# Handing seven of eight residual additions at five stage boundaries from VectorE to GpSimd

## The reference, cut to what matters

```
for l in range(2):                                   # first_block
    h = rmsnorm(x, norm_mix_pre[l])
    merged = ...                                     # pooling, convolution, attention, gates
    x = x + rmsnorm(merged @ w_out[l], norm_mix_post[l])
    h = rmsnorm(x, norm_mem_pre[l])
    x = x + rmsnorm(memory_cross_attention(h, ...), norm_mem_post[l])
    h = rmsnorm(x, norm_ffn_pre[l])
    y = (silu(conv(ua)) * ub) @ w_down[l]
    x = x + rmsnorm(y, norm_ffn_post[l])
```

## Time and profile before

| | us |
|---|---|
| median of three runs | 4000.37 |
| lowest and highest | 3993.73, 4000.42 |
| the profiled execution: time | 4001.47 |
| the profiled execution: span | 3999.7 |
| PE busy of the span | 3786.9 |
| DVE busy | 2063.7 |
| ACT busy | 1287.0 |
| POOL busy | 1203.3 |

### The profile page before, as it was taken

The page is one execution under the profiler, slowest core; times in us unless marked ns, Lnnn a source line. Parts: engine busy times, 40 slices in busy tenths (PEclk is TensorE's granted clock), DMA queues, the critical chain, the costliest instruction groups (busy, mean ns, idle before and its releaser), DMA issues. The chain is left out here.

```text
span 3999.7 us, 49029 instructions
## 1 busy us (share of the span) xinstructions
PE 3786.9 (95%) x19420; PEld 3183.6 (80%) x19420; DVE 2063.7 (52%) x3416; ACT 1287.0 (32%) x2149; POOL 1203.3 (30%) x548
## 2 busy tenths in 40 slices
PE   8999998999999998899989998899999889999999
PEld 6777776888777787688867777799999778877887
DVE  5547646565644773565456665623343566633112
ACT  4332244222433323422234443311111335543223
POOL 2224433444322443244421111122222210123443
PEclk8999999999999999999999997999999999999999
DMA  3224422333212442233321101233332200112332
GB/s 105 64 59 135 125 77 66 116 100 103 82 56 65 126 133 74 74 106 100 111 73 38 28 26 38 69 95 111 95 108 88 62 19 16 28 48 75 94 95 84
DMA packets 544449, 316.71 MB, mean 79 GB/s; under 512 B 35876, under 2 KB 517215, under 8 KB 544223
## 3 DMA queue, kind: packets, MB, share of 16 engines
q1 hardware_dynamic: 525184, 277.39, 23.9%
q10 hardware_dynamic: 19039, 36.19, 2.9%
HBM read 311.44 MB, written 2.10 MB: 78 GB/s over the span
## 5 line engine op out<-in xcount | busy, mean ns | idle before, releaser
L459 POOL TENSOR_TENSOR wlo<-wraw,whi 128x1024 fp32r<-128x1024 f32 (+6 forms) x544 | 1203.1, 2216 | 2774.9 <-ACT whi L452 2774.6
L475 PE MATMUL acc<-hh,whi 128*128 128x512 f32 (+2 forms) x2744 | 1064.1, 388 | 32.1 <-DVE hl L635 24.5
L476 PE MATMUL acc<-hl,whi 128*128 128x512 f32 (+2 forms) x2744 | 1034.7, 377 | 0.0
L477 PE MATMUL acc<-hh,wlo 128*128 128x512 f32 (+2 forms) x2744 | 1034.2, 377 | 0.0
L452 ACT ACTIVATE whi<-wraw 128x1024 fp32r<-128x1024 f32 (+6 forms) x544 | 523.7, 965 | 652.2 <-DMA wraw<-in_w_up 184.9
L475 PEld LDWEIGHTS acc<-hh,whi 128*128 128x128 f32 x2744 | 521.8, 190 | 146.8 <-issue 31.2
L476 PEld LDWEIGHTS acc<-hl,whi 128*128 128x128 f32 x2744 | 521.8, 190 | 91.5 <-issue 12.3
L477 PEld LDWEIGHTS acc<-hh,wlo 128*128 128x128 f32 x2744 | 521.0, 190 | 83.9
L1543 DVE TENSOR_TENSOR t<-acc,sq 128x768 f32<-128x768 f32 (+1 forms) x44 | 36.3, 825 | 444.3 <-PE acc L477 444.3
L475 PE MATMUL ob<-hh,whi 128*128 128x512 f32 (+3 forms) x576 | 214.3, 372 | 6.8 <-DVEq L831 6.6
L475 PE MATMUL acc<-act1h,whi 128*128 128x512 f32 x528 | 209.7, 397 | 1.4 <-DVE act1l L1551 1.4
(11 more groups left out here) (412 smaller groups left out, 6232.4 us busy)
## 6 DMA issues: line engine op xcount, KB each, us to landing
wraw<-in_ffn_w SPq DMA_DIRECT2D x120, 512.0 KB, 3.8
wraw<-in_w_in SPq DMA_DIRECT2D x102, 512.0 KB, 3.9
wraw<-in_w_up SPq DMA_DIRECT2D x88, 512.0 KB, 3.8
ada_w<-in_ada_w ACTq DMA_DIRECT2D x64, 512.0 KB, 4.1
ada_w<-in_ada_w SPq DMA_DIRECT2D x32, 512.0 KB, 4.2
wraw<-in_w_down SPq DMA_DIRECT2D x32, 512.0 KB, 4.0
wraw<-in_w_out SPq DMA_DIRECT2D x16, 512.0 KB, 4.1
wraw<-in_w_mkv SPq DMA_DIRECT2D x16, 512.0 KB, 4.0
```

The costliest lines, as they stand in the source:

```text
L459: e.tensor_tensor(wlo[0:rows, s, a:b, 0:w], wraw[0:rows, s, a:b, 0:w], whi[0:rows, s, a:b, 0:w].bitcast(F32), ALU.subtract).then_inc(lo_re ...
L475: e.matmul(o, wh, xh, start=first, stop=False)
L476: e.matmul(o, wh, xl, start=False, stop=False)
L477: return e.matmul(o, wl, xh, start=False, stop=last)
```

## The change

In the five boundaries that have a y, DVE no longer adds features 1 to 7. It makes the scaled y (`t2`) and the low half (`hl`) as before, and still adds feature 0. POOL adds the other seven, reading `t2` and `xres` and writing `xres`. Two semaphores are new: `t_scaled` tells POOL that a `t2` is there, `x_added` tells ACT that a feature is added, and tells DVE that a `t2` buffer is free again. POOL's additions come in its program after the low halves of the next stage's first two slabs and ahead of the third's. What the additions compute is the same.

```diff
+        t_scaled, x_added = sem("t_scaled"), sem("x_added")
...
+        def ends_here(T, tiles, waits, ahead=2):
+            stage_ends[len(slabs) + ahead] = (T, tiles, waits)
+
+        def pool_adds(e, c, T, tiles, waits):
+            for k in tiles:
+                e.wait_ge(t_scaled, c.next(t_scaled, waits))
+                e.tensor_tensor(xres[:, k, 0:T], xres[:, k, 0:T], t2[:, k % 2, 0:T], ALU.add).then_inc(x_added, 1)
...
-        def act_boundary(e, c, g, half=None):
+        def act_boundary(e, c, g, half=None, added=LATER):
...
-                e.wait_ge(x_ready, c.next(x_ready))
+                done = x_added if k in added else x_ready
+                e.wait_ge(done, c.next(done))
...
                 if k < KT and y is not None:
+                    if k == 2:
+                        e.wait_ge(x_ready, c.at(x_ready, 0))
+                    if k >= 3:
+                        e.wait_ge(x_added, c.next(x_added))
                     e.scalar_tensor_tensor(out=t2[:, k % 2, 0:SEQ], in0=y[:, k, :], scalar=G(k), in1=ysum[:, 0:SEQ],
-                                           op0=ALU.mult, op1=ALU.mult).then_inc(dve_step, 1)
+                                           op0=ALU.mult, op1=ALU.mult).then_inc(t_scaled if k else dve_step, 1)
+                if k == 0 and y is not None:
                     e.wait_ge(dve_step, c.next(dve_step))
                     e.tensor_tensor(xres[:, k, 0:SEQ], xres[:, k, 0:SEQ], t2[:, k % 2, 0:SEQ], ALU.add).then_inc(x_ready, 1)
...
+            if y is not None:
+                e.wait_ge(x_added, c.next(x_added, 2))
             e.wait_ge(rstd_ready, c.next(rstd_ready))
...
                 sp_cols(e, c, A["w_out"], l, KT)
+                ends_here(SEQ, LATER, 1)
...
                 sp_cols(e, c, A["w_mo"], l, 4)
+                ends_here(SEQ, LATER, 1)
                 sp_ffn(e, c, l, A["w_up"], A["w_down"])
+                if l < DEPTH - 1:
+                    ends_here(SEQ, LATER, 1)
...
             for n in range(len(slabs)):
                 tail(pool, c, n)
+                if n + 1 in stage_ends:
+                    pool_adds(pool, c, *stage_ends[n + 1])
```

More of the change, by code:

```diff
@@ L49 @@
 RES = 4
+LATER = (1, 2, 3, 4, 5, 6, 7)
 RING = 4
@@ L407, in two_blocks @@
         slabs, ada_due = [], []
+        stage_ends = {}
+        def ends_here(T, tiles, waits, ahead=2):
[4 more added lines that the diff above has]
+                e.tensor_tensor(xres[:, k, 0:T], xres[:, k, 0:T], t2[:, k % 2, 0:T], ALU.add).then_inc(x_added, 1)
         def load(e, c, parts, width=P, cols=None):
@@ L2222, in layer @@
                 e.wait_ge(gains_ready, c.next(gains_ready))
-                act_boundary(e, c, gain(0), None if l else lambda: head(e, c))
+                act_boundary(e, c, gain(0), None if l else lambda: head(e, c), added=LATER if l else ())
                 act_flow(e, c, [], tiles_1(0), one_each(tiles_1(0)), wide=True, hooks={} if l else with_mem)
```

## The result

| | before | changed |
|---|---|---|
| median, us | 3997.41 (4 runs, 3993.73 to 4000.42) | 4019.16 (4 runs, 4014.8 to 4021.9) |
| profiled execution, us | 4001.47 | 4020.62 |
| ratio, with 95% interval | | 1.0054 (1.0041 to 1.0066) |
| the same again, five runs of the changed kernel on another occasion | 3999.79 | 4025.74, 1.006 (1.0046 to 1.0074) |

The change makes the kernel slower by 0.5 to 0.6%, 22 to 26 us. The forecast was 15.0 us, to 4015.4 us, with a range that reached to 4027. It stood on the median of three runs, 4000.37; a fourth has brought that median down to 3997.41, so the time is 3.8 us above the forecast, but the rise of 21.8 us is 6.8 above it. In the last row, one of the nine runs of the kernel before took 4109.3 us at a granted clock of 0.887 and is left out of the ratio.

A forecast was written before the change was run, and what follows sets the result against it. TensorE, busy 3786.9 of 3999.7 us, bounds the kernel, but VectorE sets the pace inside boundaries. Four boundaries at 3.02 us plus 2.9 at the fifth add 15.0 to 4000.4, giving 4015.4 us, range 4004 to 4027.

The forecast's parts named there:

- The walk through the boundary: First boundary, operation by operation, GpSimd's add excluding t and low: last feature's matmuls 3.02 us later, 2.9 at the fifth.
- the pair of features: VectorE and GpSimd inside a boundary: the pattern repeats every two features, taking 4.93 us where it took 4.10.
- the add's price: GpSimd's add at boundaries: taken as 1.287 us from a subtraction of the same shape, bounded at 1.1 and 1.6.
- The hand-over of 0.08: At boundaries, 0.08 us from VectorE's end to GpSimd's start; bounds of 0 to 0.2 mean -1 to +2 in all.
- the order: At boundaries, when both engines wait, GpSimd waiting first gets in; VectorE first would give a pair of 4.95 us.
- the exclusion: At boundaries, GpSimd's add and VectorE's t or low cannot run side by side; as walked through, +8 to +20 us, chance 0.56.
- The second rival: At boundaries, the add doesn't exclude t and low: -1 to -4, about -3 us in all; chance 0.07.
- The first rival: TensorE's clock falls inside boundaries: +20 to +25 us; chance 0.28 for above +20, shared with a dearer add.
- All 15 us arrive at the end: After the boundaries nothing gives the 15 us back: the wait for the third slab's head stays, elsewhere TensorE goes straight on.
- The last term of the sum: Outside the boundaries: no gain or loss was counted beyond the boundaries' 15.0 us.
- TensorE's idle time elsewhere should be as before: Sign expected in the changed profile: outside the boundaries TensorE idles no more and no less than before.
- The room above +20 us: Upper part of the range, up to +27 us, for a falling clock or a dearer add at boundaries; chance 0.28.

The follow-up runs named there:

- the fills: Changed kernel with GpSimd's seven additions replaced by fills of the scaled y's buffer with zero, x not added for features 1 to 7: one time of 3995.31 us.
- the padded kernel: Kernel before plus one VectorE maximum of y with itself, 325 columns, for each of features 1 to 7 at the five boundaries: median 4023.97 us, ratio 1.0064.
- the factor in PSUM: Changed kernel with the factor that scales y written by ScalarE into a PSUM bank instead of SBUF tile ysum: one time of 4004.82 us.

## Why the prediction was right, and what was missing

The walk through the boundary was right to about 0.1 us in 20: low(7) ended 19.73 to 19.75 us after the first t where 19.85 was forecast, the pair of features took 16.85 - 11.95 = 4.90 us (t(5)'s end to t(7)'s) against 4.93, and the last feature came 2.8 to 2.95 us later than before against 2.9 to 3.02. In sum 14.6 us against 15.0. The small difference is mostly the add's price, 1.26 to 1.28 us where the subtraction's 1.287 was taken. The hand-over of 0.08 and the order (a waiting GpSimd gets in first) were as in the earlier trace rows.

That the exclusion is the cause is shown by the operand moved to PSUM (one half of it goes, and 1.7 of 2.95 us with it) and by the operation that reads nothing (all of it goes). The second rival, no exclusion, is out, and its -3 us a fair guess for the wrong case: 4.4 us less was what the fills gave. (One time in its working doesn't come out of its rows: five features of 1.56 us and 0.46 more from 540.87 give 549.13 and not 549.27. Nothing hangs on it.)

The Trainium skill's page "SBUF — State Buffer", section "Who interferes with whom", has the same two conditions, two SBUF inputs on VectorE and a GpSimd operation that reads SBUF, and the experiments agree. Where the same page, section "SBUF: two separate sides", lets the one that starts first keep the other out for the whole instruction, the profile's spans differ: 0.55 us of a blocked operation's 0.74 remain after the release, and GpSimd's one-input operation of 1.49 us let go after 0.60.

The first rival, the clock falling late in a boundary, didn't happen. The changed kernel's stretches from the end of the slow start to the last feature, of which the first two boundaries' are shown (columns as above, the granted clock third from the end), have a clock of 1.00 in all five, and all five boundaries agree within 0.02 us.

```profile
541.30:552.60 11.30, 9.45 (x29) 4.50 (x28) 10.24 (x10) 5.88 (x10) 5.97 (x4) 1.00 0.00 0
664.10:675.10 11.00, 9.31 (x27) 4.42 (x26) 9.97 (x9) 5.59 (x10) 5.97 (x4) 1.00 0.00 0
```

The step that failed is "All 15 us arrive at the end". They did arrive, but 22 to 26 us came in all, the other 7 to 11 from code that the change doesn't touch. The last term of the sum, what happens elsewhere, was taken as nothing ("TensorE's idle time elsewhere should be as before"), and it was the one mis-sized.

That the measured time lies inside the range is in part luck. The room above +20 us was given for two things, a clock falling inside the boundaries and an add dearer than 1.287 us, and neither happened; the 7 to 11 us that filled it came from elsewhere.

What the runs show of the excess is this. GpSimd isn't needed for it, by the padded kernel. All six comparisons of a lengthened kernel with several runs lie above the length of its boundaries, with the lower end of the interval too; the factor in PSUM, with one run, lies about 1 us below. In block 2 unchanged code is longer where the clock is at half, but this pattern doesn't follow the boundaries' length: it is there in a kernel with boundaries as short as before, and not in one with boundaries 6.2 us longer. So it isn't shown what brings the excess. That it is the place at which the clock is low, set by when TensorE comes there, is argued from a few stretches and not tested.

No variant here beats the kernel before and keeps its result. The fills say why it isn't worth more attempts: nearly free additions would bring 4.4 us, and an add on GpSimd takes 1.26 us against VectorE's 0.61 to 0.69, with VectorE's other two operations kept out meanwhile.

## What to carry to other kernels

Before moving work from VectorE to GpSimd, look for a place where they already overlap and compare durations: an operation with two SBUF inputs that takes 0.74 alone and ends 0.55 after GpSimd's is a sign that the move adds its time instead of hiding it. GpSimd's 30% share of busy time and 25 idle microseconds at the boundary promised room that wasn't there. And where TensorE is the bound, microseconds put in at one place may cost more in the end, here 12.7 for 6.1 and 28.8 for 21.0 by the medians. A sum over the changed part alone gave too small a loss each time that several runs were taken, and one profile isn't enough to say where the rest lies.

## What the runs showed of the hardware that was not expected

A GpSimd operation with one SBUF input (a multiplication of 128x512, 1.49 us) kept a VectorE operation with two SBUF inputs out only for about its first 0.60 us, while the add with two inputs (1.26 us) kept it out to the end. GpSimd's multiplication with one input took longer than its addition with two. One program had times in two heaps, 4006 and 4016 us. And unchanged code of 226.5 us at a clock of 1.00 took 230.3 at 0.97 in another kernel, although the mean clock of that whole execution wasn't lower (0.973 against 0.970).
